# A layer kernel on one Trainium2 core: the residual turned before it is normalised, router weights as the stationary side, and one turning for keys and queries

## What is computed

```python
def rms_norm(x, g):
    return x * rsqrt(mean(x * x, axis=-1) + 1e-6) * g

h = h + gated_deltanet(rms_norm(h, a_norm))                     # layer 0
h = h + moe(rms_norm(h, ffn_norm[i]))                           # both layers
#   inside moe: group logits xn @ w_rg + b (4), expert logits xn @ w_re + b (32),
#   softmax / argmax / top 2, then silu(x @ w1[e]) * (x @ w3[e]) @ w2[e]
h = h + sigmoid(rms_norm(h, ple_norm[i]) @ w_gate) * (p[i] @ w_proj)   # both layers
kv = rms_norm(h, kv_norm) @ w_kv                                # before layer 1
q  = rms_norm(h, b_norm) @ w_q                                  # layer 1, same h as kv
h = h + attention(q, kv) @ w_out
```

## Time and profile before

| | us |
|---|---|
| median of 3 runs | 1900.99 (1899.52 to 1902.57) |
| the profiled execution | 1899.08 |
| its span (first to last instruction) | 1897.3 |
| PE busy | 1791.5 (94%) |
| DVE, ACT, POOL busy | 737.3, 502.4, 106.2 |
| DMA | 488.42 MB, mean 257 GB/s |
| mean granted PE clock | 0.974 of full |

### The profile page before, as it was taken

How to read it: one execution, slowest core, us unless ns; L and a number is a source line. 1 busy time by engine, 2 the same in 40 slices (tenths; PEclk the granted TensorE clock), 3 DMA queues, 4 the chain that set the end, 5 groups by cost and what they waited for, 6 DMA issues and landing times. The chain is left out here.

```text
span 1897.3 us, 20642 instructions
## 1 busy us (share of the span) xinstructions
PE 1791.5 (94%) x7716; PEld 852.2 (45%) x7716; DVE 737.3 (39%) x1402; ACT 502.4 (26%) x757; POOL 106.2 (6%) x164
## 2 busy tenths in 40 slices
PE   7999999996999999999998999998699999999998
PEld 5555666644333333333344464555333333333343
DVE  2667444413244344343422112354334434434331
ACT  3655233312111111111212505643012112111130
POOL 0016610000000000000000000000000000000000
PEclk8999999996999999999998999999799999999999
DMA  7212322256999999999933020034899999999931
GB/s 241 70 53 74 93 78 67 76 201 234 375 422 421 421 420 421 421 421 422 411 122 133 0 96 2 0 133 173 342 415 421 421 420 421 420 422 421 421 126 45
DMA packets 108490, 488.42 MB, mean 257 GB/s; under 512 B 20096, under 2 KB 37248, under 8 KB 56960
## 3 DMA queue, kind: packets, MB, share of 16 engines
q1 hardware_dynamic: 103808, 470.59, 62.0%
q0 software_dynamic: 4608, 16.78, 2.2%
HBM read 475.28 MB, written 12.06 MB: 257 GB/s over the span
## 5 line engine op out<-in xcount | busy, mean ns | idle before, releaser
L1588 PE MATMUL bank<-ring,xT 128*64 128x512 f32 x2048 | 463.6, 599 | 14.8 <-DMA ring<-in_w 14.4
L1588 PEld LDWEIGHTS bank<-ring,xT 128*64 128x64 f32 x2048 | 141.3, 137 | 283.7 <-issue 268.6
L1540 DVE TENSOR_TENSOR H<-H,bank 128x512 f32<-128x512 f32 x240 | 160.3, 688 | 236.8 <-PE bank L1576 236.8
L1612 PE MATMUL bank<-ring,sg 128*64 128x512 f32 x1024 | 228.0, 598 | 0.0
L1576 PE MATMUL bank<-yp,Sb 128*128 128x512 bf16 x480 | 143.8, 381 | 0.0
L1612 PEld LDWEIGHTS bank<-ring,sg 128*64 128x64 f32 x1024 | 71.0, 138 | 133.7 <-issue 128.8
L446 PE MATMUL bank<-ring,ring 128*128 128x512 f32 x256 | 124.7, 596 | 0.0
L1527 DVE TENSOR_TENSOR y<-y,yp 128x512 f32<-128x512 f32 x64 | 44.3, 693 | 197.7 <-ACT yp L1637 197.7
L1628 ACT ACTIVATE sg<-bank 128x512 f32<-128x512 f32 x32 | 19.1, 597 | 380.0 <-PE bank L1597 380.0
L431 PE MATMUL bank<-ring,ring 128*128 128x512 f32 x256 | 115.1, 604 | 0.0
L1900 PE MATMUL bank<-ring,ring 128*128 128x512 f32 x256 | 111.4, 593 | 2.4 <-DVE ring L209 2.4
(11 more groups left out here) (263 smaller groups left out, 2108.0 us busy)
## 6 DMA issues: line engine op xcount, KB each, us to landing
ring<-in_w SPq DMA_DIRECT2D x192, 2048.0 KB, 29.7
ring<-in_w_heads SPq DMA_DIRECT2D x16, 1024.0 KB, 5.3
ring<-in_w_ple_gate SPq DMA_DIRECT2D x4, 2048.0 KB, 32.0
ring<-in_w_kv SPq DMA_DIRECT2D x3, 2048.0 KB, 19.5
ring<-in_b_w_q SPq DMA_DIRECT2D x3, 2048.0 KB, 13.5
inverses<-T SPq DMA_DIRECT2D x16, 256.0 KB, 4.2
ring<-in_a_w_out SPq DMA_DIRECT2D x2, 2048.0 KB, 7.9
rows<-ring SPq DMA_DIRECT2D x8, 512.0 KB, 11.5
```

Source lines behind the costliest of these rows:

```text
L1540: dve.tensor_tensor(out, out, k.bank[6 + j % 2][:, :], ALU.add).then_inc(s.added, 1)
L1588: last = pe.matmul(out[e * SLOTS:(e + 1) * SLOTS, :], k.xT[:, at, e * SLOTS:(e + 1) * SLOTS], w[:, e, c, :], start=(at == 0), stop=(at == ...
L1612: last = pe.matmul(k.bank[2 + n][e * SLOTS:(e + 1) * SLOTS, :], k.hT[:, c, e * SLOTS:(e + 1) * SLOTS], w[:, e, c % 2, n * HALF:(n + 1) * H ...
```

## The change

Routing and embedding turn the raw `H`, not `xn` (`turn_residual`), so PE can start before the norm is known; the gain is still applied at the evacuation, and the division by the deviation comes later: for routing at the addition of the bias (`scalar_tensor_tensor` with `rstd`), for the embedding in the sigmoid's `scale`. In routing the rows `xn` for the gather are made after the evacuations. The router's weights become the stationary side: 8 products with 36 output partitions and 512 moving columns, even chunks into partitions 0 to 35 of one bank and odd ones into 64 to 99 of another; ACT and DVE copy both to `by_expert`, and 4 products with a two-part identity (`both`, made by POOL) add the halves and turn them back to tokens. In attention the keys' evacuation becomes two operations: a copy of the bank to `xhT`, then the gain from `xhT` to `xnT`; after the keys ACT multiplies `xhT` by the queries' gain in place, and the queries read that. The 32 turnings and 8 evacuations before the queries go. `xhT` takes the memory of `xn`, and the attention's scratch moves to that of `xnT`.

The diff, cut to its core:

```diff
+def squares_scalar(act, k, s, t):
+    act.activation(k.xn[:, t, :], k.H[:, t, :], ACT.Square, accum_out=k.ss[:, t:t + 1]).then_inc(s.ss, 1)
...
+def raw_chunk_vector(dve, k, s, c, gain, banks):
+    dve.wait_ge(s.turned, c + 1)
+    dve.tensor_scalar(k.xnT[:, c, :], k.bank[c % banks][:, :], gain[:, c:c + 1], None, ALU.mult).then_inc(s.xnT, 1)
...
+def turn_residual(pe, k, s, banks):
+    for c in range(DC):
+        if c >= banks:
+            norm_chunk(pe, s, c - banks)
+        for t in range(NT):
+            last = pe.transpose(k.bank[c % banks][:, t * P:(t + 1) * P], k.H[:, t, c::DC], k.ident)
+        last.then_inc(s.turned, 1)
...
-        norm_scalar(act, k, s, k.g_kv)
+        norm_scalar_rows(act, k, s)
+        for c in range(1, DC, 2):
+            act.wait_ge(s.turned, c + 1)
+            act.activation(k.xhT[:, c, :], bank[c][:, :], ACT.Copy).then_inc(s.xh_odd, 1)
+            act.wait_ge(s.xh_odd, c // 2 + 1)
+            act.activation(k.xnT[:, c, :], k.xhT[:, c, :], ACT.Copy, scale=k.g_kv[:, c:c + 1]).then_inc(s.xnT_odd, 1)
         for j in range(self.heads):
             square(act, k, s, j, bank[j % 4])
             if j:
                 root(act, k, s, j - 1, bank[4 + (j - 1) % 2])
         root(act, k, s, self.heads - 1, bank[4 + (self.heads - 1) % 2])
+        act.wait_ge(s.xnT, DC // 2)
+        for c in range(DC):
+            act.activation(k.xhT[:, c, :], k.xhT[:, c, :], ACT.Copy, scale=k.g_b[:, c:c + 1]).then_inc(s.xq, 1)
...
-        norm_vector(dve, k, s, k.g_kv)
+        norm_vector_rows(dve, k, s)
+        for c in range(0, DC, 2):
+            dve.wait_ge(s.turned, DC if c == DC - 2 else c + 1)
+            dve.tensor_copy(k.xhT[:, c, :], bank[c][:, :]).then_inc(s.xh, 1)
+            dve.wait_ge(s.xh, c // 2 + 1)
+            dve.tensor_scalar(k.xnT[:, c, :], k.xhT[:, c, :], k.g_kv[:, c:c + 1], None, ALU.mult).then_inc(s.xnT, 1)
...
-                        norm_chunk(pe, q, c)
-                    last = pe.matmul(bank_of(n)[:, :], w[:, c, :], k.xnT[:, c, :], start=(c == 0), stop=(c == DC - 1))
+                        pe.wait_ge(kv.xq, c + 1)
+                    if n == 2 and c == 0:
+                        pe.wait_ge(kv.v, 2 * NT)
+                    last = pe.matmul(bank_of(n)[:, :], w[:, c, :], k.xhT[:, c, :], start=(c == 0), stop=(c == DC - 1))
...
-            pe.wait_ge(kv.v, 2 * NT)
-            norm_tensor(pe, k, q, fresh=False)
...
 def route_tensor(pe, k, s, layer):
-    norm_tensor(pe, k, s)
-    norm_chunk(pe, s, 2)
-    norm_chunk(pe, s, 3)
+    turn_residual(pe, k, s, DC)
     for c in range(DC):
         norm_chunk(pe, s, c)
-        for t in range(NT):
-            last = pe.matmul(k.bank[t][:, 0:MG + EXPERTS], k.xnT[:, c, t * P:(t + 1) * P],
-                             k.w_router[:, layer, c, :], start=(c == 0), stop=(c == DC - 1))
-    last.then_inc(s.logits, 1)
+        last = pe.matmul(k.bank[c % 2][c % 2 * ODD:c % 2 * ODD + LOGITS, :], k.w_router[:, layer, c, :], k.xnT[:, c, :],
+                         start=(c < 2), stop=(c >= DC - 2), skip_group_check=True)
+    last.then_inc(s.sums, 1)
+    pe.wait_ge(s.both, 1)
+    pe.wait_ge(s.even, 1)
+    pe.wait_ge(s.odd, 1)
+    for t in range(NT):
+        pe.matmul(k.bank[2 + t][:, 0:LOGITS], k.by_expert[0:ODD + LOGITS, t * P:(t + 1) * P], k.both[0:ODD + LOGITS, :],
+                  start=True, stop=True).then_inc(s.logits, 1)
...
-    norm_scalar(act, k, s, k.g_ffn[:, layer, :])
+    gain = k.g_ffn[:, layer, :]
+    for t in range(0, NT, 2):
+        squares_scalar(act, k, s, t)
+        raw_chunk_scalar(act, k, s, t + 1, gain, DC)
+    deviation(act, k, s)
+    for c in range(5, DC, 2):
+        raw_chunk_scalar(act, k, s, c, gain, DC)
+    act.wait_ge(s.rstd, 1)
+    for t in range(1, NT, 2):
+        act.activation(k.xn[:, t, :], k.H[:, t, :], ACT.Copy, scale=k.rstd[:, t:t + 1]).then_inc(s.xn_odd, 1)
+    act.wait_ge(s.sums, 1)
+    act.wait_ge(s.cleared, 1)
+    act.activation(k.by_expert[0:LOGITS, :], k.bank[0][0:LOGITS, :], ACT.Copy).then_inc(s.even, 1)
...
-    norm_vector(dve, k, s, k.g_ffn[:, layer, :])
+    gain = k.g_ffn[:, layer, :]
+    for t in range(1, NT, 2):
+        squares_vector(dve, k, s, t)
+        raw_chunk_vector(dve, k, s, t - 1, gain, DC)
+    variance(dve, k, s, NT // 2, NT // 2)
+    raw_chunk_vector(dve, k, s, 4, gain, DC)
+    inverse_deviation(dve, k, s)
+    raw_chunk_vector(dve, k, s, 6, gain, DC)
+    dve.wait_ge(s.rstd, 1)
+    for t in range(0, NT, 2):
+        dve.tensor_scalar(k.xn[:, t, :], k.H[:, t, :], k.rstd[:, t:t + 1], None, ALU.mult).then_inc(s.xn, 1)
+    dve.wait_ge(s.sums, 1)
+    odd = slice(ODD, ODD + LOGITS)
+    dve.tensor_copy(k.by_expert[odd, :], k.bank[1][odd, :]).then_inc(s.odd, 1)
     ch = s.chain = Chain(dve, s.steps)
     places = k.place.rearrange("p (t s) -> p t s", t=NT)
     dve.tensor_copy(k.aux[:, :, :, 0:2], bcast(places, 2, PAIRS)).then_inc(s.places, 1)
-    dve.wait_ge(s.logits, 1)
     for t in range(NT):
-        logits = dve.tensor_tensor(lg[:, t, :], k.bank[t][:, 0:MG + EXPERTS], k.b_router[:, layer, :], ALU.add)
+        dve.wait_ge(s.logits, t + 1)
+        logits = dve.scalar_tensor_tensor(lg[:, t, :], k.bank[2 + t][:, 0:LOGITS], k.rstd[:, t:t + 1],
+                                          k.b_router[:, layer, :], ALU.mult, ALU.add)
...
+def route_pool(pool, k, s):
+    pool.memset(k.by_expert[32:ODD, :], 0.0).then_inc(s.cleared, 1)
+    pool.wait_ge(s.cleared, 1)
+    pool.tensor_tensor(k.both[:, :], k.ident[:, 0:LOGITS], k.ident[:, ODD:ODD + LOGITS], ALU.add).then_inc(s.both, 1)
...
-    norm_tensor(pe, k, s, chunks=range(4), banks=4)
-    norm_tensor(pe, k, s, chunks=range(4, DC), banks=4)
-    norm_chunk(pe, s, DC - 2)
-    norm_chunk(pe, s, DC - 1)
+    pe.wait_ge(s.settled, 1)
+    turn_residual(pe, k, s, 4)
+    norm_chunk(pe, s, DC - 4)
+    norm_chunk(pe, s, DC - 3)
...
+                if j < 4 and c == 0:
+                    norm_chunk(pe, s, (DC - 4 + j) % DC)
+                if j == 0:
+                    norm_chunk(pe, s, c)
...
-    norm_scalar(act, k, s, k.g_ple[:, layer, :], fresh=False, banks=4)
+    for c in range(1, DC, 2):
+        raw_chunk_scalar(act, k, s, c, k.g_ple[:, layer, :], 4)
+    act.wait_ge(s.rstd, 1)
...
-        act.activation(k.sg[:, j % 2, :], k.bank[j % 4][:, :], ACT.Sigmoid).then_inc(s.sig, 1)
+        act.activation(k.sg[:, j % 2, :], k.bank[j % 4][:, :], ACT.Sigmoid,
+                       scale=k.rstd[:, j % NT:j % NT + 1]).then_inc(s.sig, 1)
...
-            norm_vector_rows(dve, k, e, settled, by_vector)
+            dve.sem_inc(e.settled, 1)
+            for t in by_vector:
+                squares_vector(dve, k, e, t)
+            variance(dve, k, e, len(by_scalar), len(by_vector))
+            inverse_deviation(dve, k, e)
...
-                k.aoT = k.ring2[:, 1, 0:QPG * SEQ].rearrange("p (h n) -> p h n", h=QPG)
-                k.PTa = k.ring2[:, 1, 4096 - SEQ:]
-                k.sc = k.ring2[:, 1, QPG * SEQ:QPG * SEQ + 2 * NSCORE].rearrange("p (b n) -> p b n", b=2)
+                k.xhT = k.ring2[:, 1, :].rearrange("p (c n) -> p c n", c=DC)
+                k.aoT = k.ring2[:, 0, 0:QPG * SEQ].rearrange("p (h n) -> p h n", h=QPG)
+                k.PTa = k.ring2[:, 0, 4096 - SEQ:]
+                k.sc = k.ring2[:, 0, QPG * SEQ:QPG * SEQ + 2 * NSCORE].rearrange("p (b n) -> p b n", b=2)
```

More of the change, by code:

```diff
@@ L106 @@
 GATE = 0
+LOGITS, ODD = MG + EXPERTS, 64
 def piece_slot(q, m):
@@ L226, in norm_vector_rows, with squares_vector, variance, deviation @@
         dve.tensor_scalar(k.xn[:, t, :], k.H[:, t, :], k.rstd[:, t:t + 1], None, ALU.mult).then_inc(s.xn, 1)
+def squares_scalar(act, k, s, t):
+    act.activation(k.xn[:, t, :], k.H[:, t, :], ACT.Square, accum_out=k.ss[:, t:t + 1]).then_inc(s.ss, 1)
+def squares_vector(dve, k, s, t):
+    dve.tensor_tensor_reduce(k.xn[:, t, :], k.H[:, t, :], k.H[:, t, :], 1.0, 0.0, ALU.mult, ALU.add,
+                             accum_out=k.ss[:, t:t + 1]).then_inc(s.ss_odd, 1)
+def variance(dve, k, s, by_scalar, by_vector):
+    dve.wait_ge(s.ss_odd, by_vector)
+    dve.wait_ge(s.ss, by_scalar)
+    dve.tensor_scalar(k.var[:, :], k.ss[:, :], 1.0 / D, EPS, ALU.mult, ALU.add).then_inc(s.var, 1)
+def deviation(act, k, s):
+    act.wait_ge(s.var, 1)
+    act.activation(k.std[:, :], k.var[:, :], ACT.Sqrt).then_inc(s.std, 1)
+def inverse_deviation(dve, k, s):
+    dve.wait_ge(s.std, 1)
+    dve.reciprocal(k.rstd[:, :], k.std[:, :]).then_inc(s.rstd, 1)
+def raw_chunk_scalar(act, k, s, c, gain, banks):
+    act.wait_ge(s.turned, c + 1)
+    act.activation(k.xnT[:, c, :], k.bank[c % banks][:, :], ACT.Copy, scale=gain[:, c:c + 1]).then_inc(s.xnT_odd, 1)
+def raw_chunk_vector(dve, k, s, c, gain, banks):
[8 more added lines that the diff above has]
+        last.then_inc(s.turned, 1)
 def norm_tensor(pe, k, s, fresh=True, chunks=range(DC), banks=DC):
@@ L903, in feature_semaphores @@
     s = norm_semaphores(k, tag)
```

(19 more changed lines are left out.)

6 lines of the change are left out of this document (3 added, 3 removed).

## The result

The changed kernel takes 1876.79 us (median of 4 runs, 1873.84 to 1881.86), the kernel before 1901.78 (4 runs, 1899.52 to 1902.77): ratio 0.9879, 95% interval 0.9861 to 0.9897. The profiled execution took 1879.15, its span is 1877.4 (1899.08 and 1897.3 before).

A forecast was written before the change was run, and what follows sets the result against it. Each expert stage was taken to end with its weight stream, embedding and attention with PE's start. Routing 13.8 + embedding 6.5 + attention 4.8 - 0.4 = 24.7 us off 1899.08 gives 1874.4, predicted median 1875.5; range 1869 to 1881, 8 in 10 1866 to 1885.

The forecast's parts named there:

- The total: Whole kernel: 24.7 us won against the profiled 1899.08, predicted as a median of 1875.5 us; chance 0.58.
- Logits: Routing until the last bias: earlier turnings and wide router products bring logits 13.2 us earlier in layer 0, 10.4 in layer 1.
- Stores and gather level: Routing: row stores keep their landing and come out level with `index`; gathers issued at 458.0 and 1332.0.
- The gather: First gather takes 8.9 us beside two pieces in flight, landing 8.6 and 5.2 us earlier, 13.8 together.
- The whole stage behind it moves along.: Expert stage: it shifts by as much as the first gather's landing, 13.8 us over both layers.
- Embedding: Embedding: turning the raw residual starts gate products 3.3 us earlier in layer 0 and 3.2 in layer 1, 6.5 together.
- Attention: Attention: 4.8 us won between values and queries, 0.4 us lost at the keys.
- the 0.4 us of the two-step evacuation: Attention keys: copy then gain makes only the first key product late, by 0.4 us.
- A: Rival: the gather overtakes the pieces in its queue and takes 4.3 us, 9.2 us more won: 1866; chance 0.14.
- B: Rival: PE's clock falls in routing, wide products take 7 us, gathers come 2.5 to 3 us later: 1880.5; chance 0.15.
- C: Rival: stores land late behind slot 9, routing gives only about 3 us for both layers: 1885; chance 0.08.
- D: Rival: changed logit rounding lifts an expert over 64 tokens, so `more_experts` runs a whole pass: 2352; chance 0.02.

The follow-up runs named there:

- attend_only: Kernel before with only the attention part of the change: 1893.87 us, ratio 0.9969 to the kernel before.
- stores_by_pool: Changed kernel with slot 6 loaded after the first gather and the four `xn` stores issued by GpSimd instead of SP: 1879.74 us, 0.9893 of the kernel before.
- gather_first_2: Second run of the changed kernel with slot 6 loaded only after the first gather: 1871.03 us, 0.9840 of the kernel before.
- whole_again: The changed kernel, unaltered, run again: 1874.69 us, ratio 0.9865 to the kernel before.
- whole_third: The changed kernel, unaltered, run a third time: 1875.82 us, ratio 0.9863 to the kernel before.
- gather_alone: Changed kernel with slots 6 and 9 both loaded only after the first gather: 1880.99 us, ratio 0.9892 to the kernel before.
- gather_first: Changed kernel with one wait moved, so slot 6 is loaded only after the first gather: 1873.91 us, ratio 0.9851 to the kernel before.

## Why the prediction was right, point by point

- **The total.** 1875.5 predicted, 1876.79, 1874.69 and 1875.82 measured; the sum of 24.7 us stands against 25.0 between the medians, and 23.3, 25.4 and 24.2 by stages in the three traces. That it is as near as this is partly luck: the errors of the stages, below, cancel, and one execution of before differs from the next by more than the miss (runs of 1896 to 1906).
- **Logits.** Turnings at the block's start at clock 1.00 (3.80 and 3.83 us, forecast 3.7), the 8 wide products in 3.63 us (forecast 3.5, side by side), bias 9.6 and 9.6 us after the start (forecast 10.2). Won on the logits: 13.8 and 11.1 us, forecast 13.2 and 10.4. I took these two for the layers' own; `attend_only` shows that they change places with the clock.
- **Stores and gather level.** The gather was released by the stores in both layers, 20.1 and 18.9 us after the start (forecast 19.3 and 19.7). Right as a mechanism, also in the last store's landing, which I left where it was: 19.1 and 18.1 us after the start, 18.5 and 19.3 before. The reason was incomplete. I had the two pieces ahead done 10 us after the block's start; the second one landed after 13.5 us (455.46; 12.5 before), and the four stores, 2 MB together, came in behind it until 461.15. In `stores_by_pool`, with slot 9 ahead of them too, the last one landed another 3.7 and 4.3 us later than in `gather_first_2`.
- **The gather.** Forecast 8.9, measured 9.5 and 10.3 (8.7 to 10.3 in the three runs of the changed kernel). The landing gained 7.3 and 4.8 us where the sum had 8.6 and 5.2. In layer 0 the issue came 0.8 us late and the gather took 0.6 longer; in layer 1 the issue came 0.8 early and the gather took 1.4 longer.
- **"The whole stage behind it moves along."** This step is mis-sized, and its reason is imprecise. The block's gain less the embedding was 6.3 and 3.9 = 10.2 us where the sum had 13.8; about half of the missing 3.6 us was lost up to the landing, the rest behind it. From the landing to the last pair PE took 0.7 us more in each layer in this trace (0.5 more, 0.2 less in `whole_again`; 0.9 and 0.8 more in `whole_third`), and the embedding's second part with the barrier took 0.1 to 0.2 more. So here the stage nearly did move along. That it must is wrong: in `gather_alone` the landing came 4.3 and 5.2 us earlier than in the changed kernel, and the blocks were 2.8 and 2.1 us longer, because the stream stood still. I took slot 6 to keep the stream full up to the gather. It did until about 470 (share 0.90 in 468 to 470), but the gather was slow beside it, and slots 7 and 0 wait for the gather; the two holes of 470 and 478 are the result. `gather_first` closes the second one and gains though it loads less ahead.
- **Embedding.** Forecast 3.3 and 3.2, measured 4.2 and 3.9, at the early bound of 4.0: PE turned at 948.35, as its queue came to it, without the 1.3 us that I left open. Together 8.0 where the sum had 6.5. The gate products began 3.6 us after the first turning, as forecast. The sigmoid's mean is 0.69 instead of 0.60 us, and from the first gate product to the embedding's end it is 0.1 us longer.
- **Attention.** Forecast 4.4, measured 5.0 (5.4 to 5.8 in `whole_again`, `whole_third` and `attend_only`). No gap between values and queries. The keys' first product came 10.45 us after the block's start (10.47 before), so the 0.4 us of the two-step evacuation cost nothing: PE's turnings, at half clock for the most part, ended at 1028.60, and the chunk followed 0.63 later. The 0.4 us that the sum took off were not lost.
- **Rivals.** A (a quick gather) is out for the changed kernel, where it took 8.7 to 10.3 us. `gather_first` gets a quick gather by holding slot 6 back, and 3.5 to 4.7 us on the landing gave only 1.3 to 2.5 on the stage. B happened in part, in 4 of the 10 layer 0 routings, for the turnings alone, at 1.5 us on the logits instead of 3 and at most 0.7 us on the gather's issue. C and D did not occur: the stores landed in time, and the experts' part has no second pass.

The errors (routing -3.6, embedding +1.5, attention +0.6) partly cancel.

## What to carry to other kernels

When a stage ends with a stream of weights, the worth of an earlier start is how much more the DMA has moved by then, and the landing of the first input stands for that only while the order of the loads stays the same; read the mean GB/s over the stage's first stretch before and after, times its length, and divide the difference by the full rate. In these kernels that came within 1.1 us but for two blocks. A small transfer on the critical path is slow for what is queued ahead of it, so here its wait belongs ahead of the big load's issue, but only one load deep: the second load held back, 2 MB or 5.0 us at 421 GB/s, cost 6.0 and 4.3 us (`gather_alone`). A DMA moved to another queue frees what stood behind it, and that may go ahead of it (`stores_by_pool`). Before a stage's time is compared, look at its granted clock in more than one execution: the kernel before had 3 us more in one of two equal routings (0.59 against 0.71). The fastest version that computes everything is `gather_first`, at 0.984 and 0.985.
